# A chain of eight transformer stages on one core: row tile 1 turned later, the last product of a stage opened by the next one's first products, and weight splits moved behind them

## What is computed

```python
def first_block(h):
    # layer 0: short convolution mixer, then feed-forward
    b, c, u = split(rms(h) @ w_in, 3)
    h = h + rms((b * causal_conv3(c * u)) @ w_out)
    h = h + rms((silu(g) * up) @ w_down)            # g, up = split(rms(h) @ w_gate_up, 2)
    # layer 1: attention over a window of 128 with sinks, then feed-forward
    k, v = split(rms(h, kv_norm) @ w_kv, 2); q = rotary(rms(h, b_pre_norm) @ w_q)
    h = h + rms(window_attention(q, rotary(k), v, sinks) @ w_o)
    return h + rms((silu(g) * up) @ w_down)

def second_block(h):
    h = h + 0.5 * swiglu(rms(h))
    parts = rms(h) @ w_in                           # 2464 columns: latent q, latent kv, rope key, retention q k v g
    h = h + concat(latent_attention(parts), retention(parts)) @ w_o
    h = h + 0.5 * swiglu(rms(h))
    return rms(h, final_norm)
```

## Time and profile before

| | |
|---|---|
| median of 3 executions | 1075.31 us (1074.78 to 1075.59) |
| profiled execution, its own time | 1074.11 us |
| its span, first to last instruction | 1072.2 us |
| PE busy in the span | 1055.5 us (98%) |
| DVE busy | 655.8 us (61%) |
| ACT busy | 560.9 us (52%) |
| DMA, mean | 175 GB/s |

### The profile page before, as it was taken

How to read it: one execution, slowest core, us unless ns; L and a number is a source line. 1 busy time by engine, 2 the same in 40 slices (tenths; PEclk the granted TensorE clock), 3 DMA queues, 4 the chain that set the end, 5 groups by cost and what they waited for, 6 DMA issues and landing times.

```text
span 1072.2 us, 14824 instructions
## 1 busy us (share of the span) xinstructions
PE 1055.5 (98%) x5047; PEld 872.1 (81%) x5047; DVE 655.8 (61%) x930; ACT 560.9 (52%) x907; POOL 101.4 (9%) x194
## 2 busy tenths in 40 slices
PE   9999999999999999999999999999999999999997
PEld 6898888888787788888888888887888888888886
DVE  5867654545787864554666455466568674645543
ACT  5756544544667664444555444455476534444542
POOL 0034000000012041000001000000027120000001
PEclk9999999999999999999999999999999999999999
DMA  8664546556561454645565465556545133646541
GB/s 337 197 232 157 181 160 210 181 171 215 196 196 61 136 180 159 223 165 196 192 205 174 157 225 158 202 194 215 159 157 177 61 122 114 202 165 220 162 152 40
DMA packets 51884, 187.81 MB, mean 175 GB/s; under 512 B 5808, under 2 KB 5952, under 8 KB 51840
## 3 DMA queue, kind: packets, MB, share of 16 engines
q1 hardware_dynamic: 50688, 183.79, 51.3%
q0 software_dynamic: 864, 3.07, 0.8%
q10 hardware_dynamic: 288, 0.37, 0.1%
HBM read 186.15 MB, written 1.05 MB: 175 GB/s over the span
## 4 chain that ended last, share of the span: by engine, by line
PE 89%; DVE 6%; ACT 2%; issue 1%; DMA 1%; POOL 0%; POOLq 0%; ACTq 0%; DVEq 0%; SPq 0%
PE pG L1629 16%; PE pG L1631 16%; PE pG L1630 16%; PE pD L1629 11%; PE pD L1631 11%; PE pD L1630 11%; PE pT L1634 3%; DVE w_low L1295 3%; PE pG L1651 1%; PE pG L1634 1%; PE pT L1945 1%; PE pG L1932 1%; ACT w_high L1026 1%; PE pD L1906 1%; PE pT L1772 1%
## 5 line engine op out<-in xcount | busy, mean ns | idle before, releaser
L1295 DVE TENSOR_TENSOR w_low<-raw,w_high 128x1024 fp32r<-128x1024 f32 x340 | 412.5, 1232 | 118.8 <-ACT w_high L1026 105.3
L1026 ACT ACTIVATE w_high<-raw 128x1024 fp32r<-128x1024 f32 x340 | 352.5, 1055 | 79.4 <-PE pG L1631 67.6
L1629 PE MATMUL pG<-w_high,xTh 128*128 128x512 f32 (+1 forms) x816 | 319.9, 392 | 1.7 <-DVE xTl L1328 1.6
L1631 PE MATMUL pG<-w_high,xTl 128*128 128x512 f32 (+1 forms) x816 | 312.4, 383 | 0.0
L1630 PE MATMUL pG<-w_low,xTh 128*128 128x512 f32 (+1 forms) x816 | 312.1, 382 | 0.0
L1631 PEld LDWEIGHTS pG<-w_high,xTl 128*128 128x128 f32 x816 | 153.1, 188 | 28.0
L1629 PEld LDWEIGHTS pG<-w_high,xTh 128*128 128x128 f32 x816 | 153.2, 188 | 27.8 <-DVE xTl L1328 2.6
L1630 PEld LDWEIGHTS pG<-w_low,xTh 128*128 128x128 f32 x816 | 153.5, 188 | 25.6
L1629 PE MATMUL pD<-w_high,aTh 128*128 128x512 f32 x384 | 151.0, 393 | 2.4 <-DVE aTl L1433 2.4
L1631 PE MATMUL pD<-w_high,aTl 128*128 128x512 f32 x384 | 149.9, 390 | 0.0
L1630 PE MATMUL pD<-w_low,aTh 128*128 128x512 f32 x384 | 149.4, 389 | 0.0
(11 more groups left out here) (266 smaller groups left out, 827.7 us busy)
## 6 DMA issues: line engine op xcount, KB each, us to landing
raw<-in_stream SPq DMA_DIRECT2D x340, 512.0 KB, 4.3
post<-in_posts POOLq DMA_DIRECT2D x5, 512.0 KB, 4.9
early<-in_stream SPq DMA_DIRECT2D x4, 512.0 KB, 12.5
first_w<-in_stream SPq DMA_DIRECT2D x3, 512.0 KB, 6.0
h<-in_x SPq DMA_DIRECT2D x2, 512.0 KB, 5.6
out<-hg SPq DMA_DIRECT2D x3, 256.0 KB, 2.5
consts<-in_consts POOLq DMA_DIRECT2D x1, 416.0 KB, 4.7
out<-hg ACTq DMA_DIRECT2D x1, 256.0 KB, 2.7
```

The lines of the kernel that those rows point to most:

```text
L1026: sc.activation(w_high[:, slot(static):slot(static) + CHUNK], raw_of(static), ACT.Copy).then_inc(w_high_done, 1)
L1295: ve.tensor_tensor(w_low[:, slot(static):slot(static) + CHUNK], raw_of(static), w_high[:, slot(static):slot(static) + CHUNK].bitcast(F32), ...
L1629: pe.matmul(dst, ah, hi, start=start, stop=False)
L1631: return pe.matmul(dst, al, hi, start=False, stop=stop)
```

## The change

Five things are moved in the list of steps, and one piece of arithmetic moves from ACT to DVE.

1. Mixer to FFN1: three splits leave the end of the mixer (its block 6). They come later: two behind `Y 1 7`, two behind `T 0 0` of FFN1, then `join 1`, then four.
2. In the last block of FFN1, FFN2 and FFN3 two splits instead of three stand ahead of `G 1 10`, and three behind `T 1 10` as before, so that one comes later.
3. FFN1 to attention and FFN3 to latent stage: the first projections of row tile 0 now stand ahead of `D 1 10`, `turn 1` stands behind the first product of the second group for row tile 0 (`proj 1 0 0`, `X 1 0 0`), and `second 0` directly behind the tail.
4. Attention to FFN2: one split instead of four ahead of `turn 0`, four instead of two behind `O 1 6`.
5. FFN2 to FFN3: one split between `T 0 0` and `join 1`, the rest behind it.
6. `finish`: the squares of the last 256 columns are summed by DVE with a `tensor_tensor_reduce` that starts from EPS, no longer by ACT.

```diff
@@ walk_block_step
     if s == 0 and open_end:
         open_end()
         step("T", 0, 0, shift)
+        refill(step, freed, 2 if ph is FFN1 else 1)
+        step("join", 1, ph.index - 1)
         refill(step, freed)
-        step("join", 1, ph.index - 1)
         return
@@ walk_follower
-    if ph.mixer:
+    if ph.mixer and b == ph.nb - 2:
+        freed += [*range(g + early, g + ph.cg), ph.d_chunk(b - 1)]
+    elif ph.mixer:
         step("R", g + early, ph.cg - early, shift)
     if not first:
         step("T", 1, b, shift)
-    if not first and not last:
+    if not first and not last and not (ph.mixer and b == ph.nb - 2):
         step("R", ph.d_chunk(b - 1), ph.kd, shift)
@@ walk_last_follower
-    early = 0 if ph.mixer else 3
+    early = 0 if ph.mixer else 2
...
+    freed += [*range(g + early, g + ph.cg), *range(ph.d_chunk(b - 1), ph.d_chunk(b - 1) + ph.kd)]
     step("T", 1, b, 0)
     if ph.mixer:
         step("Y", 1, b, 0)
-    freed += [*range(g + early, g + ph.cg), *range(ph.d_chunk(b - 1), ph.d_chunk(b - 1) + ph.kd)]
-    refill(step, freed, 3)
+    refill(step, freed, 2 if ph.mixer else 3)
@@ walk_attention
-    projects(0, 0, range(3))
+    project(0, 0, 0)
+    open_end()
+    step("second", 0)
+    projects(0, 0, range(1, 4))
+    step("join", 1, FFN1.index)
+    project(1, 0, 0)
     walk_prep(step, 1, B_INDEX)
-    project(0, 0, 3)
-    step("second", 0)
     refill(step, freed)
+    projects(1, 0, range(1, 4))
     projects(0, 1)
     step("second", 1)
     refill(step, freed, 2)
-    projects(1, 0)
     step("rope", 0, 0)
     refill(step, freed)
     step("exp_table",)
@@ end of walk_attention
     output(1, 4)
-    refill(step, freed, 4)
+    refill(step, freed, 1)
     walk_prep(step, 0, B_INDEX + 1)
     for kt in range(5, 7):
         output(1, kt)
-    refill(step, freed, 2)
+    refill(step, freed, 4)
@@ walk_latent
-    projects(0, 0)
+    projects(0, 0, range(2))
+    open_end()
+    step("join", 1, FFN3.index)
+    projects(0, 0, range(2, 4))
+    refill(step, freed, 1)
+    project(1, 0, 0)
     walk_prep(step, 1, C_INDEX)
-    refill(step, freed, 2)
-    projects(1, 0)
+    refill(step, freed)
+    projects(1, 0, range(1, 4))
     step("LAT", 0)
@@ finish, ACT
-                sc.wait_ge(h_ready[1], 2 * (LAST - 1) + 3)
-                sc.activation(junk[1][:, fourth], h[1][:, fourth], ACT.Square, scale=D ** -0.5,
-                              accum_out=ss_end).then_inc(ss_ready[1], 1)
@@ finish, DVE
+                ve.wait_ge(h_ready[1], 2 * k + 3)
+                chain(ve.tensor_tensor_reduce(junk[1][:, fourth], h[1][:, fourth], h[1][:, fourth], 1.0 / D, EPS, ALU.mult, ALU.add, ss_end))
+                joined()
                 ve.wait_ge(ss_ready[1], 2 * LAST + 2)
-                chain(ve.tensor_scalar(ms[1], ss[1][:, 0:1], ss[1][:, 1:2], EPS, ALU.add, ALU.add))
+                chain(ve.tensor_scalar(ms[1], ss[1][:, 0:1], ss[1][:, 1:2], None, ALU.add))
                 joined()
-                ve.wait_ge(ss_ready[1], 2 * LAST + 3)
                 ve.tensor_scalar(ms[1], ms[1], ss_end, None, ALU.add).then_inc(end_m, 1)
```

More of the change, by code:

```diff
@@ L279, in walk_phase, with walk_attention @@
     walk_last_follower(ph, step, freed)
-def walk_attention(step, freed):
+def walk_attention(step, freed, open_end):
     def project(j, t, c):
@@ L395, in walk_attention, with walk_latent @@
         output(1, kt)
-    refill(step, freed, 2)
-def walk_latent(step, freed):
+    refill(step, freed, 4)
+def walk_latent(step, freed, open_end):
     def project(i, t, c):
@@ L544, in walk @@
     walk_phase(eng, FFN1, lambda *a: step(*a, ph=FFN1), 4, freed, lambda: end_of(MIX))
-    end_of(FFN1)
-    step("join", 1, FFN1.index)
-    walk_attention(lambda *a: step(*a, ph=None), freed)
+    walk_attention(lambda *a: step(*a, ph=None), freed, lambda: end_of(FFN1))
     walk_phase(eng, FFN2, lambda *a: step(*a, ph=FFN2), 4, freed, end_of_attention)
     walk_phase(eng, FFN3, lambda *a: step(*a, ph=FFN3), 4, freed, lambda: end_of(FFN2))
-    end_of(FFN3)
-    step("join", 1, FFN3.index)
-    walk_latent(lambda *a: step(*a, ph=None), freed)
+    walk_latent(lambda *a: step(*a, ph=None), freed, lambda: end_of(FFN3))
     walk_phase(eng, FFN4, lambda *a: step(*a, ph=FFN4), 3, freed)
@@ L1077, in finish @@
             def finish(ph):
-                left, right, third, fourth = slice(0, 512), slice(512, 1024), slice(512, 768), slice(768, 1024)
+                left, right, third = slice(0, 512), slice(512, 1024), slice(512, 768)
                 square(0, LAST, 0)
@@ L1373, in finish @@
                 added(1, fourth, pT[0][:, 0:256])
+                ve.wait_ge(h_ready[1], 2 * k + 3)
+                chain(ve.tensor_tensor_reduce(junk[1][:, fourth], h[1][:, fourth], h[1][:, fourth], 1.0 / D, EPS, ALU.mult, ALU.add, ss_end))
+                joined()
                 ve.wait_ge(ss_ready[1], 2 * LAST + 2)
-                chain(ve.tensor_scalar(ms[1], ss[1][:, 0:1], ss[1][:, 1:2], EPS, ALU.add, ALU.add))
+                chain(ve.tensor_scalar(ms[1], ss[1][:, 0:1], ss[1][:, 1:2], None, ALU.add))
                 joined()
-                ve.wait_ge(ss_ready[1], 2 * LAST + 3)
                 ve.tensor_scalar(ms[1], ms[1], ss_end, None, ALU.add).then_inc(end_m, 1)
-                ve.wait_ge(h_ready[1], 2 * k + 3)
                 weighted(1, left).then_inc(end_w, 1)
```

## The result

The change makes the kernel slower: 1078.08 us (1077.36 to 1079.59, 8 executions) against 1075.14 us (1074.54 to 1075.87, 8 executions), a ratio of 1.0029 with the interval 1.0018 to 1.0040. Forecast was +1.8 us, measured are +2.9 in the medians and +3.9 between the two profiled spans (1072.2 and 1076.1). The profiled execution before, with 1074.11, lay 1.0 under its median; the one after, with 1077.92, lay 0.2 under its own.

The account below looks back on a forecast made before the run. PE's work plus idle time bounds the kernel; terms +3.1 + 1.3 - 1.5 - 0.5 - 0.25 - 0.25 = +1.9, stated as +1.8, put 1075.31 at 1077.1 us; forecast band 1076.5 to 1078.0, ends 1074.3 and 1079.1.

Parts of the forecast that it names:

- FFN1's start: Mixer to FFN1: late act of G 0 1 delays G 1 0, gain already included; +3.1 us, +2.2 to +3.7.
- attention: FFN1 to attention: removed waits gain 2.0, uncovered x2l wait costs 2.25, scores come 1.3 later; +1.3 us, +0.25 to +2.3.
- attention to FFN2: Three low parts go behind the turned tile's gain on DVE, removing the wait at 375.94; -1.5 us, -1.5 to -0.5.
- FFN2 to FFN3: One low part less ahead of act on DVE removes the wait at 562.12; -0.5 us.
- latent stage: FFN3 to latent: the wait at 750.25 is covered, a wait for lat adds 0.85; -0.25 us, -1.1 to +0.1.
- final norm: DVE sums the squares itself instead of waiting for ACT; -0.25 us, -0.65 to +0.2.
- the 3.3 of the rival: Rival "hardly felt", chance 0.30: the least landing of 3.3 us speaks for chunk 40's load not being late; 1076.2 us.
- The prediction's 3.2 us: Estimated transfer time of 512 KB by the skill page; with it the FFN1-start term is +2.2 and the sum 0.9 lower.
- the point X: FFN1 to attention: PE has issued all of proj 0 1 3, at 311.5 in the new order; then x2h_104's product waits.
- the fall behind the two gaps at FFN1's start: Rival "the clock falls", chance 0.05: ten or more products cost 0.2 us more each, +2 or more, 1079.3 us.
- the right gain at FFN1's start: G 0 1 starts at 111.2 instead of 112.60, gain 1.4 us; one split less ahead of join 0 hides turn 0's wait.

Follow-up runs that it names:

- one-split variant: Changed kernel with one split instead of three taken from the mixer's block 6, one between join 1 and act, chunk 40 behind T 0 1: 1073.21 us, ratio 0.9978.
- the one with the mixer undone: Changed kernel with the mixer-to-FFN1 part as before the change, everything else as changed: 1073.06 us beside 1074.82, ratio 0.9981.
- the one with one split behind: Changed kernel with only the split of chunk 40 moved from ahead of act of G 0 1 to behind T 0 1: 1074.65 us, ratio 0.9996.
- two variants: Kernel before with only the mixer-to-FFN1 part: 1078.99 us; changed kernel with two of four groups proj 1 0 c behind second 1 again: 1075.63 us.
- both-mended kernel: Changed kernel with the one-split variant's mixer end and two of four groups proj 1 0 c behind second 1: 1069.80 us beside 1074.94, ratio 0.9950.

## Why the prediction was right or wrong

**The number.** 1078.08 us is 1.0 above the 1077.1 of the forecast, just outside the forecast's own band (1076.5 to 1078.0), and above 1077.46, where it had put a chance of 0.39. That it came so near is in part luck: without the clock the stretches add up to +1.2, 0.6 less than the forecast +1.8, and the clock, which had no term, brought back that and more.

**Right:** the direction, and stretch by stretch the waits: FFN1's start +2.73 (forecast +3.1), attention +1.18 (+1.3), attention to FFN2 -1.56 (-1.5), FFN2 to FFN3 -0.59 (-0.5), latent stage -0.27 (-0.25), final norm -0.26 (-0.25). The load of chunk 40 took the 4.4 us that the sum used, not the 3.3 of the rival. (The prediction's 3.2 us is worked out from a fit that the page of the Trainium skill gives for transfers of gpsimd; SyncE issues these.) `act` began at 122.12, against 122.5 worked out, since everything behind `turn 0` ran 0.3 us ahead. In the attention the point X, where PE had issued all of `proj 0 1 3`, came at 316.9, which is the 311.5 worked out and the 5.4 us brought along, with 2.18 us to the next product (2.25 forecast). The `tensor_tensor_reduce` took 0.43 and 0.08 us.

**Wrong: the clock was left out of the sum.** The forecast named the fall behind the two gaps at FFN1's start as a rival with a chance of 0.05 and a price of +2 or more. It came, for 2.67 us in the profiled execution, and the mean clock of all eight executions was 0.995 or 0.996, where the kernel before has 0.998 or 0.999 in its executions beside the experiments (once 0.997). The reason given against it was that gaps of up to 1.6 us had left the clock at 1.00. Those stand alone; here two of 1.8 and 1.55 stand with only two transposes between them. Filling either with useless products, with nothing else moved, kept the clock up in the profiled execution, and filling the first took 1.9 us off the kernel: the idle time does it.

**Wrong: which split held `join 0`.** The forecast had the right gain at FFN1's start and the wrong split. The one-split variant kept the wait of 1.13 us. What held `join 0` was `yT` behind the pair of low parts: with one of the pair behind `yT` the wait was gone, and `T 0 1` came 1.1 us earlier.

**Left open.** Whether a single gap of about 2 us takes the clock. Six profiled kernels have the wait of 2.02 us in the attention: behind it the clock stayed up in the changed kernel and in the two with filled gaps, and fell for seven products in the one with the mixer undone, the one-split variant and the one with one split behind. What decides it was not tried. The final norm's 0.26 us and the latent stage's 0.27 us are read from traces, too small for the times.

## What to carry to other kernels

A transposed tile, a norm or an activation that is late costs its wait once, and when two such waits stand close together they can cost the clock as well: here a `G 1 0` that came 2.7 us late brought 1.5 to 2.7 us of slow products with it, and a wait is worth more to remove than its length. Before work is deferred out of one stage, count what the receiving engine must then do ahead of the first instruction that the bound engine needs there, with the loads that deferring holds up; three splits of 1.2 us were too many, one was free. And look not for the last instruction ahead of the late one but for the last that was not itself waiting: the low part right in front of the norm stood in idle time, the pair two steps ahead did not.

## What was unexpected of the hardware

- A gap pays twice: the half clock outlasted the idle time, which had ended at 124.64, by 13 products (5.7 us, of which 2.7 were lost) in the changed kernel's trace. It is not a fixed price: 1.5 and 1.6 us were lost at the same place in the traces of two variants.
- The first 55 us of the program, which no edit touches, differ by up to 1.6 us between profiled executions: the same transposes of the mixer stood at 54.3 us in the both-mended kernel and at 55.9 in the one-split variant. So spans of single executions can't be compared to better than this, unless the traces agree there (before and after do, to 0.08 us); distances between two points of one trace can.
- Loads that the change held up and then released 1.15 us apart, at 117.9, 119.0 and 120.2, took 7.0 to 7.1 us each to landing, where 5.0 was the most before. The 512 KB of norm gains that GpSimd loads were in flight beside them; that this and not their own number made them slow was not tried. They were needed later: PE has no wait from behind the start of `G 1 0` to 142 us. The changed kernel's transfers into `raw` from 110 to 124 us:

```profile
DMA to landing us min/median/max: 3.4/6.2/7.1
```
